# Low-rank products of decay, rate and output gate as rounded passes of split operands, with the splits made in the r, k, v stage

## What is computed

```python
p = p + (_shift(p, 1) - p) * mu
r, k, v, wd, ad, gd = jnp.split(p, splits, axis=-1)      # wd, ad: 64 columns each, gd: 160
w_raw = -jax.nn.softplus(-(w0 + jnp.tanh(wd) @ w_lora_up)) - 0.5   # decay, 64 x 512
a = jax.nn.sigmoid(a0 + ad @ a_lora_up)                            # rate, 64 x 512
g = jax.nn.sigmoid(gd) @ g_lora_up                                 # output gate, 160 x 512
...
return (yn + bonus) * g                                  # yn: y after the group norm
```

## Time and profile before

| what | value |
|---|---|
| time, median of 3 runs | 3748.15 us (3746.01 to 3752.31) |
| the profiled execution: its own time | 3749.11 us |
| its span in the profile | 3747.3 us |
| granted PE clock over the span | 0.985 of full |
| PE busy / DVE / POOL / ACT | 95% / 63% / 39% / 35% |

### The profile page before, as it was taken

The page is one execution under the profiler, slowest core; times in us unless marked ns, Lnnn a source line. Parts: engine busy times, 40 slices in busy tenths (PEclk is TensorE's granted clock), DMA queues, the critical chain, the costliest instruction groups (busy, mean ns, idle before and its releaser), DMA issues. The chain is left out here.

```text
span 3747.3 us, 69598 instructions
## 1 busy us (share of the span) xinstructions
PE 3570.6 (95%) x29231; PEld 3307.2 (88%) x29231; DVE 2372.4 (63%) x2813; ACT 1314.7 (35%) x1902; POOL 1471.7 (39%) x847
## 2 busy tenths in 40 slices
PE   6999999999999999999998999999999999999998
PEld 6767988988898999999986689888869989999997
DVE  2364447565559877776834643585655697777676
ACT  5343124222213444353443420441231144444435
POOL 5364930000252655543443669000004435655341
PEclk9999999999999999999999999999999999999999
DMA  5431765432322222273334238563324122222732
GB/s 119 127 80 47 245 212 184 134 78 80 117 82 74 75 86 74 80 256 123 87 71 127 60 117 252 176 189 108 82 70 145 48 86 86 74 80 85 255 121 84
DMA packets 475734, 438.12 MB, mean 117 GB/s; under 512 B 105835, under 2 KB 400967, under 8 KB 475447
## 3 DMA queue, kind: packets, MB, share of 16 engines
q1 hardware_dynamic: 455192, 382.22, 34.0%
q10 hardware_dynamic: 20255, 51.78, 3.8%
HBM read 296.88 MB, written 137.05 MB: 116 GB/s over the span
## 5 line engine op out<-in xcount | busy, mean ns | idle before, releaser
L280 POOL TENSOR_TENSOR w_hi<-w_raw,consts 128x1024 fp32r<-128x1024 f32 (+1 forms) x78 | 128.1, 1642 | 1197.0 <-DMA w_raw<-in_w_proj_rwkv 832.0
L234 PE MATMUL psum<-h_hi,w_hi 128*128 128x348 f32 x1632 | 353.8, 325 | 11.3 <-ACT lat_sq L860 3.8
L234 PE MATMUL psum<-h_lo,w_hi 128*128 128x348 f32 x1632 | 348.3, 322 | 0.0
L234 PE MATMUL psum<-h_hi,w_lo 128*128 128x348 f32 x1632 | 347.9, 322 | 0.0
L234 PEld LDWEIGHTS psum<-h_hi,w_hi 128*128 128x128 f32 x1632 | 274.3, 189 | 19.5 <-POOL w_lo L282 4.6
L234 PEld LDWEIGHTS psum<-h_lo,w_hi 128*128 128x128 f32 x1632 | 276.6, 188 | 0.0
L234 PEld LDWEIGHTS psum<-h_hi,w_lo 128*128 128x128 f32 x1632 | 275.1, 188 | 0.0
L3197 POOL TENSOR_TENSOR piece_lo_w<-sum,piece_hi_w 128x512 fp32r<-128x512 f32 x120 | 209.2, 1743 | 139.7 <-ACT piece_hi_w L3510 136.7
L3242 PE MATMUL psum<-t_hi,piece_hi_w 128*128 128x260 f32 x1280 | 258.4, 283 | 4.2 <-DVE t_lo L3749 2.6
L3242 PE MATMUL psum<-t_lo,piece_hi_w 128*128 128x260 f32 x1280 | 258.1, 283 | 0.0
L3242 PE MATMUL psum<-t_hi,piece_lo_w 128*128 128x260 f32 x1280 | 257.1, 282 | 0.0
(11 more groups left out here) (618 smaller groups left out, 9623.3 us busy)
## 6 DMA issues: line engine op xcount, KB each, us to landing
w_raw<-in_w_in SPq DMA_DIRECT2D x68, 512.0 KB, 9.6
wsum<-in_w_down SPq DMA_DIRECT2D x88, 256.0 KB
wsum_scratch<-wsum SPq DMA_DIRECT2D x22, 1024.0 KB
raw_g<-in_w_up SPq DMA_DIRECT2D x40, 512.0 KB, 3.8
raw_v<-in_w_up SPq DMA_DIRECT2D x40, 512.0 KB, 3.8
gate_scratch<-gst ACTq DMA_DIRECT2D x32, 522.0 KB, 3.0
gbuf<-gate_scratch SPq DMA_DIRECT2D x32, 522.0 KB, 3.5
prep_scratch<-prep ACTq DMA_DIRECT2D x8, 2080.0 KB, 8.3
```

The costliest lines, as they stand in the source:

```text
L234: last = nc.tensor.matmul(bank[:, n, :], w(k), x(k)[:, nrange(n)], start=(k == 0 and q == 0), stop=(k == kt - 1 and q == 2))
L280: nc.gpsimd.tensor_tensor(w_hi[s][:, 0:width], w_raw[s][:, 0:width], consts[:, 4:5].broadcast_to([P, width]), ALU.mult).then_inc(hi_done.s ...
```

## The change

Decay and rate. The rounded high part of `lora_x` goes to `xw` (rows 0 to 63) and `xa` (rows 64 to 127), the low part is copied by DMA to the other 64 rows of the same tile. The weights are loaded twice, in both halves, and rounded (`ww_hi`, `aa_hi`), with their low parts in `up_low`. One product is then two rounded passes: one over 128 rows (high and low of x by the high part of w) and one over 64 rows (high of x by low of w). Output gate: high and low parts of `gd0` and of the weights are stored in DRAM (`gd_parts`, `wg_parts`), the 32 rows of `gd1` are stacked as three groups in 96 rows; they are loaded again at the end of the scan stage and in the group norm, and one `G` is four rounded passes in place of six float32 calls. All splits are made in the r, k, v stage, ahead of ACT's and DVE's loops. The buffers of the gate stage begin at `base` instead of `rwkv_base`. The low x low products are left out.

```diff
+        def up_product(bank, s, j):
+            part, x, w = (WD, AD)[s], (xw, xa)[s], (ww_hi, aa_hi)[s]
+            cols = slice(j * P, (j + 1) * P)
+            for n in range(NB):
+                nc.tensor.matmul(bank[:, n, :], w[:, cols], x[:, nrange(n)], start=True, stop=False)
+            for n in range(NB):
+                last = nc.tensor.matmul(bank[:, n, :], up_low[part, cols], x[part, nrange(n)], start=False, stop=True)
+            return last
...
             def _(sp):      # r, k, v stage
+                def low_rank_weights():
+                    for half in (WD, AD):
+                        sp.dma_start(ww_raw[half, :], a["w_lora_up"][l]).then_inc(up_in, 16)
+                        sp.dma_start(aa_raw[half, :], a["a_lora_up"][l]).then_inc(up_in, 16)
+                    sp.dma_start(wg_raw[:, :], a["g_lora_up"][l, 0:P, :]).then_inc(up_in, 16)
+                    for n in range(3):
+                        sp.dma_start(w96_raw[n * G1:(n + 1) * G1, :], a["g_lora_up"][l, P:GATE_LORA, :]).then_inc(up_in, 16)
+
+                def low_rank_parts():
+                    sp.wait_ge(dpre.sem, dpre.of(0, "l96"))
+                    sp.dma_start(xw[AD, :].bitcast(F32), x_low[WD, :].bitcast(F32)).then_inc(lora_in, 16)
+                    sp.dma_start(xa[WD, :].bitcast(F32), x_low[AD, :].bitcast(F32)).then_inc(lora_in, 16)
+                    sp.dma_start(gd_parts[0], g0_hi[:, :].bitcast(F32)).then_inc(parts_out, 16)
+                    sp.dma_start(gd_parts[1], g0_lo[:, :].bitcast(F32)).then_inc(parts_out, 16)
+                    for n in range(2):
+                        sp.dma_start(gd_parts[2, n * G1:(n + 1) * G1], g1_hi[G1R, :].bitcast(F32)).then_inc(parts_out, 16)
+                    sp.dma_start(gd_parts[2, 2 * G1:3 * G1], g1_lo[G1R, 1:TP + 1].bitcast(F32)).then_inc(parts_out, 16)
+                    sp.dma_start(wg_parts[0], wg_hi[:, :].bitcast(F32)).then_inc(parts_out, 16)
+                    sp.dma_start(wg_parts[1], wg_lo[:, :].bitcast(F32)).then_inc(parts_out, 16)
+                    sp.dma_start(wg_parts[2, 0:3 * G1], w96[0:3 * G1, :].bitcast(F32)).then_inc(parts_out, 16)
...
                 for u in range(nt):
                     load_unit(sp, u + 2, u % 2, loaded, split, [(kview(KD), w_in_v[:, :, u * P:(u + 1) * P])])
+                    if u == 0:
+                        low_rank_weights()
+                    elif u == 4:
+                        low_rank_parts()
...
-                sp.dma_start(w_l[0:DECAY_LORA, :], a["w_lora_up"][l, :, 0:P]).then_inc(lora_in, 16)
-                sp.dma_start(w_l[DECAY_LORA:P, :], a["a_lora_up"][l, :, 0:P]).then_inc(lora_in, 16)
+                sp.wait_ge(parts_out, 16 * NSPLIT)
...
             def _(act):     # r, k, v stage, after the sigmoids and ahead of the loop
+                act.wait_ge(apre.sem, apre.of(0, "sg1"))
+                apre.did(nc.scalar.activation(xw[WD, :], lora_x[WD, :], ACT.Copy), "hxw")
+                apre.did(nc.scalar.activation(xa[AD, :], lora_x[AD, :], ACT.Copy), "hxa")
+                apre.did(nc.scalar.activation(g0_hi[:, :], gd0[:, :], ACT.Copy), "hg0")
+                apre.did(nc.scalar.activation(g1_hi[G1R, :], gd1[G1R, 1:TP + 1], ACT.Copy), "hg1")
+                act.wait_ge(up_in, 16 * NSPLIT)
+                apre.did(nc.scalar.activation(ww_hi[:, :], ww_raw[:, :], ACT.Copy), "hww")
...
             def _(dve):     # r, k, v stage, ahead of the loop
+                def low(dst, raw, high, hi_name, name):
+                    dve.wait_ge(apre.sem, apre.of(0, hi_name))
+                    dpre.did(nc.vector.tensor_tensor(dst, raw, high, ALU.subtract), name)
+                low(x_low[WD, :], lora_x[WD, :], xw[WD, :], "hxw", "lxw")
+                low(x_low[AD, :], lora_x[AD, :], xa[AD, :], "hxa", "lxa")
+                low(g0_lo[:, :], gd0[:, :], g0_hi[:, :], "hg0", "lg0")
+                low(g1_lo[G1R, 1:TP + 1], gd1[G1R, 1:TP + 1], g1_hi[G1R, :], "hg1", "lg1")
+                low(up_low[WD, :], ww_raw[WD, :], ww_hi[WD, :], "hww", "lww")
...
             def _(sp):      # gate stage: lora(j) and its two DMAs are gone
-                        lora(j + 1)
                         mixed(j + 1)
...
             def _(pe):      # gate stage
                     if j:
-                        pe.wait_ge(w_got, j * 32 + 32)
                         pe.wait_ge(dves.sem, dves.of(0, f"bon{j - 1}"))
-                        pes.did(product32(one, [(w_l[0:DECAY_LORA, :], lora_x[0:DECAY_LORA, :])]), f"zw{j}")
+                        pes.did(up_product(one, 0, j), f"zw{j}")
...
             def _(act):     # gate stage, j = 0, ahead of the first write to prep
+                        act.wait_ge(rkv_landed[l], 16 * (3 * RT // 2 + 1))
...
             def _(sp):      # end of the scan stage, after the last chunk's loads
+                for n in range(3):
+                    rows = slice(0, P if n < 2 else 3 * G1)
+                    sp.dma_start(g_part[n][rows, :].bitcast(F32), gd_parts[n, rows]).then_inc(parts_in, 16)
+                sp.wait_ge(parts_in, 16 * 3)
...
             def _(pe):      # group norm, the four products G
-                    for n in range(NB):
-                        bank = pset[(j + 1) % 2][:, n, :]
-                        nc.tensor.matmul(bank, wg0[:, j * P:(j + 1) * P], gd0[:, nrange(n)], start=True, stop=False)
-                        last = nc.tensor.matmul(bank, wg1[grows, j * P:(j + 1) * P], gd1[grows, 1 + n * NW:1 + (n + 1) * NW], start=False, stop=True)
+                    cols = slice(j * P, (j + 1) * P)
+                    for q, (w, x) in enumerate(((0, 0), (0, 1), (1, 0), (2, 2))):
+                        rows = g96 if q == 3 else slice(0, P)
+                        for n in range(NB):
+                            last = nc.tensor.matmul(pset[(j + 1) % 2][:, n, :], w_part[w][rows, cols], g_part[x][rows, nrange(n)], start=(q == 0), stop=(q == 3))
```

More of the change, by code:

```diff
@@ L2303, in layer @@
         gsq = gt
-        wg0 = after("wg0", [P, RW])
-        wg1 = after("wg1", [P, RW])
+        w_part = [after(f"w_part{n}", [P, RW], F32R) for n in range(3)]
         gn_end = cursor[0]
@@ L2309, in layer @@
         grs = place("grs", [P, RT, TP], F32, TOP + 4 * RT * TP)
-        grows = slice(ROPE, ROPE + G1)
+        g96 = slice(0, 3 * G1)
         z = place("z", [P, KD, TP], F32, base)
```

86 lines of the change are left out of this document (58 added, 28 removed).

## The result

The changed kernel took 3774.9 us (median of 4 runs) beside 3747.1 us for the kernel before: ratio 1.008, 95% interval 1.0065 to 1.0095, so 27.8 us slower. It was run twice more, each time with the kernel before beside it: 1.0054 (1.0035 to 1.0073) and 1.0068 (1.0053 to 1.0083), 20.6 and 26.8 us slower. The forecast was 11.7 us slower: right in sign, less than half of the size.

What follows compares the result with a forecast made beforehand. PE is busy 95% of the span; in the r, k, v stage PE and POOL run in lockstep. Terms -1.4 + 0 + 10.7 + 1.4 + 1.0 = +11.7 us on 3749.11 give 3760.8, as a median 3759.8 us; range 3746 to 3777.

Steps and rivals of the forecast that it cites:

- DVE's eight subtractions, +10.7: In the r, k, v stage: they slow POOL, 0.89 us per long one, half per short; +10.7 us for two layers.
- The eight weight DMAs, +1.4: r, k, v stage, unit 0: w_down blocks come late, POOL waits about 0.7 us per layer; +1.4 us, bounds 0 and 8.6.
- 370 to 371: r, k, v stage, unit 0: assumed time of the w_down blocks' arrival before the change; POOL starts on them at 372.57.
- The ten DMAs at unit 4, +1.0: r, k, v stage: 2.7 MB ahead of unit 2's store, mostly absorbed by POOL's delay; +1.0 us, bounds -3 and +14.
- Rival 2: DMA queues become the bound in the r, k, v stage, 12 to 16 us longer per layer; 3774 us, chance 0.17.
- G 0: Group norm: G products shrink from 18.6 to 7.6 us per layer beside DVE's chain; 0 us won, lower bound -22.
- the pair -1.4: Gate stage: shorter decay and rate products win only the waits of `sw`; -1.4 us, bounds -8 and 0.
- Rival 5: Products don't get shorter if a pass costs over 0.475 us; time stays as forecast; chance 0.45 together with the main case.
- rival 4: Group norm: idle PE drops to its lower clock, 2 to 3 us per layer on top, 3765 us; chance 0.08.
- ACT's eight roundings, 0: r, k, v stage: 6.5 us of roundings delay the first copy-out from 388.3 to about 395; cost nothing.

Runs made afterwards that it cites:

- one late store without a byte: Kernel before with one added wait: at unit 4 SP holds the store of unit 2's sums until unit 3's sums are done; 3764.9 us, ratio 1.0054.
- the exchange of two lines: Sums' store issued ahead of the w_in load in each unit: changed kernel 3768.4 us, ratio 1.0061; kernel before 3742.1 us, ratio 0.9989.
- G twice: Changed kernel with the four passes of each output-gate product made twice; one run, stage 168.8 / 174.3 us, group norm stretch 38.6 and 38.5 us.
- the two changed kernels with the store ahead: Changed kernel with sums' store ahead of the w_in load, ratio 1.0061; the same with unit 4's ten transfers behind store and loads, ratio 1.0045.

## Why the prediction was wrong in size

**DVE's eight subtractions, +10.7: right.** Measured alone 9.7 (5.2 and 4.5), within the bounds 7.2 to 15. The price of 0.89 us for each, from two units of POOL, was good. The port rule of the Trainium skill (SBUF — State Buffer, "Who interferes with whom"), taken to the letter, gave 7.5 per layer; the run shows two thirds of that, and the measurement decides.

**The eight weight DMAs, +1.4: too small.** The waits they leave (1.50 and 3.04 us) are like the 0.7 per layer only in kind: the blocks had stood closer to their use than the "370 to 371" that I put. In the stage it is 2.6 and 3.9 us, 6.5 in all and inside the bound of 8.6. This rests on one profile; the runs give 3.4 us with an interval that holds none.

**The ten DMAs at unit 4, +1.0: the step that failed.** They cost POOL 12.7 us between the fourth and the tenth unit; with the terms above at 9.7 and 6.5, 8.9 of the stages' 25.1 us are left for them. I reckoned a delay that happens once and that POOL's own lateness takes in ("What is left shortens the lead of the loads"). But the lead is no stock that is drawn on once: each store that is late is issued right behind the loads, lands in 8.4 to 11.0 us in place of 5.1 to 6.5, and makes the next load late. The rows that said so were in the trace before the change, late in the stage:
```profile
471.07 1.76 SPq L1459 DMA_DIRECT2D wsum<-in_w_down  x4
...
473.37 1.92 SPq L1463 DMA_DIRECT2D wsum_scratch<-wsum  x1
483.27 2.30 SPq L1459 DMA_DIRECT2D wsum<-in_w_down  x4
```
There the store already leaves right behind the two loads and takes 9.9 us. Rival 2 had the place, and its test ("waits for `w_down` blocks beyond 5 us per layer") came true with 12.7 to 24.4; its size, 3774, was near too. Its mechanism, the amount that the queues have to move, was at most half of it: one late store without a byte costs as much, and the exchange of two lines took the waits away with all bytes in place. Yet order isn't all either. Between the fourth and the tenth unit the exchange brings the changed kernel from 12.7 to 2.9 us, but the kernel before to -3.4, so 6.3 of the cost stay there, and over the whole stage the change costs as much in the new order as in the old. What makes up the rest is open.

**The float32 products: G 0, right; the pair -1.4, not shown.** G took 11.1 us of PE (4.25 + 6.84) in place of 18.6, more than my 7.6 since the second block ran at the lower clock. That won nothing, nor did G twice lose anything; the chain of DVE, 960.02 to 980.4, is as long as before (20.4 us, and 20.3 from 2789.86 to 2810.2). The pair is hardly shorter, for a pass of it is 0.68 us from start to start, not 0.475 (changed kernel, PE, j = 2):
```profile
629.21 0.75 PE L1466 MATMUL psum<-xw,ww_hi 128*128 128x348 f32 x3
629.89 0.75 PE L1468 MATMUL psum<-xw,up_low 64*128 64x348 f32 x3
630.57 0.74 PE L1466 MATMUL psum<-xa,aa_hi 128*128 128x348 f32 x3
631.24 0.74 PE L1468 MATMUL psum<-xa,up_low 64*128 64x348 f32 x3
631.91 2.02 PE L266 MATMUL psum<-sqn,head_ones 128*128 128x348 f32 x6
```
`ss` starts 2.70 us after the pair, where it was 3.16: the wait for `sw`, which I had expected to grow to over 1 us, is gone, and 0.46 us with it. The gate stage is 0.9 and 1.1 us shorter in the first profile, but in the kernels whose gate stage is that of before it lies between 401.9 and 406, so this gain can't be told. Rival 5 was true of the pair, and as it said, without effect.

**PE's clock (rival 4): it fell, and cost nothing.** Stretches of layer 0 in the changed kernel: length, busy time (instructions) of PE, PEld, DVE, ACT, POOL, granted clock, DMA share, GB/s:
```profile
962.90:969.70 6.80, 5.70 (x18) 5.27 (x19) 6.69 (x6) 2.15 (x2) 0.00 (x0) 0.50 0.01 2
973.20:976.60 3.40, 3.40 (x13) 3.40 (x13) 3.33 (x3) 0.80 (x1) 0.00 (x0) 0.52 0.00 0
```
The clock fell to its lower level, 1.2 GHz, during the wait of 3.74 us for `gt`, was back at full from 970.9 to 973.0, and was at the lower level again behind the wait of 2.16; the passes at 972.99 take 0.9 us each in place of 0.475. The rule of the Trainium skill (TensorE: Matmul & The Clock Gate, "Why this matters for your kernels"), that idle gaps between bursts of matmuls bring the lower clock, agrees with the row behind the 3.74 us. Yet PE is through at 977.6 and waits for `y_lo` until 979.22 as before: the slow passes fill the gap that the short G left.

**ACT's eight roundings, 0: right by the rows.** The first copy-out starts at 394.36 in the changed kernel, and I had forecast 395.

## What to carry to other kernels

Where a load waits for a store to land and both share one queue with other loads, write down the circle in the order of issue, with two landing times for the store: alone, and right behind the loads. If the second makes the circle longer than the consumer's period, a single delay isn't paid once but can stay for many units. Then try the store ahead of every load that doesn't depend on it, and try it in the kernel before as well: here it helped both alike, and only the pair of runs tells that. And work saved on the busiest engine is worth nothing where another engine's chain spans the same stretch, while in a stage whose two engines run in lockstep what a small operation takes from one of them is paid at the stage's end.

## What the runs showed of the hardware

- A store of 1 MB of sums that left over 3 us behind the last load landed 5.1 to 6.5 us after its issue (kernel before). On the same queue, right behind 1 MB of loads, it took 7.6 to 8.4 us (four stores of the two changed kernels with the store ahead), and right behind 1.5 MB 8.4 to 11.0 (36 stores in three profiles of the changed kernel).
- The same program has a stage of 169.1 to 175.5 us, from run to run and from layer to layer, as the circle of store and load comes back to its time or doesn't.
- Two-input subtractions of DVE over 1044 columns took 2.2 us beside POOL's sums in place of 1.25, and POOL's sums of 512 columns 2.2 to 2.3 in place of 1.29.
- Matmul passes of the low-rank pair, which change tiles and row counts each time, start 0.68 us apart, while passes of 128 rows in the same stage start 0.475 apart, with the clock at full in both.
